# Opening of a trunk layer by feature halves: modulation, weights and the first two projections taken for features 0-511, then for 512-1023

## The reference

```python
sh1, sc1, g1, sh2, sc2, g2 = split(silu(c) @ w_mod + b_mod, 6)     # w_mod: 1024 x 6144, f32
hn   = rms_norm(x, norm1_w) * (1 + sc1) + sh1
proj = hn @ w_in                                                   # w_in: 1024 x 2832, f32
q_a, k_a, v_a, q_m, k_m, v_m, o_m, gates = split(proj, ...)
# attention and a two-direction mLSTM over proj, then @ w_out, x = x + g1 * y
# second norm with sh2, sc2; router over 64 experts (top 8), 192 MB of expert weights, x + g2 * moe
```

## Time and profile before

| what | value |
|---|---|
| median of 3 executions | 644.04 us |
| span of the profiled execution | 642.9 us |
| PE busy | 580.9 us (90% of the span) |
| DVE, ACT, POOL busy | 209.8, 168.1, 33.6 us |
| DMA | 252.55 MB, mean 393 GB/s |
| chain that ended last | PE 63%, DMA 28%, SP's queue 3% |
| mean granted PE clock | 0.975 |

### The profile page before, as it was taken

How to read it: one execution, slowest core, us unless ns; L and a number is a source line. 1 busy time by engine, 2 the same in 40 slices (tenths; PEclk the granted TensorE clock), 3 DMA queues, 4 the chain that set the end, 5 groups by cost and what they waited for, 6 DMA issues and landing times.

```text
span 642.9 us, 11139 instructions
## 1 busy us (share of the span) xinstructions
PE 580.9 (90%) x4568; PEld 405.9 (63%) x4568; DVE 209.8 (33%) x474; ACT 168.1 (26%) x309; POOL 33.6 (5%) x79
## 2 busy tenths in 40 slices
PE   0789999999999999989999999587999999998785
PEld 0478777788867676656675757354567676765352
DVE  0287867787832212011212222020121212121103
ACT  3164726672622121111121212010212121212111
POOL 1240210010100000000000000000000000000002
PEclk9989999999999999999999999788999999999879
DMA  8999599989999899999999999999999999999994
GB/s 334 385 339 392 208 363 383 411 317 396 420 378 374 365 415 411 422 422 420 420 421 422 420 420 421 421 422 421 420 422 421 419 421 421 421 421 420 421 399 168
DMA packets 50662, 252.55 MB, mean 393 GB/s; under 512 B 5912, under 2 KB 11680, under 8 KB 26288
## 3 DMA queue, kind: packets, MB, share of 16 engines
q1 hardware_dynamic: 48240, 246.37, 94.5%
q0 software_dynamic: 1840, 4.21, 2.0%
q10 hardware_dynamic: 528, 1.21, 0.5%
HBM read 250.06 MB, written 1.72 MB: 392 GB/s over the span
## 4 chain that ended last, share of the span: by engine, by line
PE 63%; DMA 28%; SPq 3%; ACT 2%; DVE 2%; issue 1%; POOL 0%; POOLq 0%; DVEq 0%; ACTq 0%
PE bank L1265 22%; PE bank L1341 11%; DMA spare<-in_w_up 7%; PE bank L1236 6%; PE bank L1282 5%; DMA xn<-in_w_up 4%; DMA gb<-in_w_down 4%; DMA ring<-in_w_up 4%; DMA ring<-in_w_in 4%; DMA ring<-in_w_mod 2%; PE bank L834 2%; SPq L617 2%; PE bank L876 2%; PE bank L884 2%; PE bank L880 2%; DMA ccol<-in_c 2%
## 5 line engine op out<-in xcount | busy, mean ns | idle before, releaser
L1265 PE MATMUL bank<-ring,xe 128*64 128x256 f32 (+1 forms) x1680 | 179.4, 398 | 22.9 <-DMA ring<-in_w_up 8.2
L1265 PEld LDWEIGHTS bank<-ring,xe 128*64 128x64 f32 (+1 forms) x1680 | 118.0, 131 | 79.3 <-issue 44.8
L1341 PE MATMUL bank<-ring,actT 128*64 128x512 f32 (+1 forms) x368 | 83.6, 617 | 4.2 <-DVE actT L2313 2.1
L2311 DVE TENSOR_TENSOR act_e<-bank,sil 128x256 f32<-128x256 f32 x26 | 11.0, 424 | 188.2 <-ACT sil L1727 188.2
L2325 DVE SCALAR_TENSOR_TENSOR ylo<-bank,gslot,yhi 128x512 fp32r<-128x512 f32 x50 | 37.5, 750 | 83.6 <-ACT yhi L1740 83.6
L1740 ACT ACTIVATE yhi<-bank,gslot 128x512 fp32r<-128x512 f32 x50 | 34.4, 688 | 116.1 <-PE bank L1341 116.1
L1727 ACT ACTIVATE sil<-bank 128x256 f32<-128x256 f32 x26 | 10.0, 385 | 192.1 <-PE bank L1265 192.1
L1236 PE MATMUL bank<-pone,hhi 128*128 128x256 f32 x200 | 50.0, 288 | 0.0
L1341 PEld LDWEIGHTS bank<-ring,actT 128*64 128x64 f32 (+1 forms) x368 | 24.5, 132 | 39.2 <-issue 38.9
L1236 PE MATMUL bank<-pone,hlo 128*128 128x256 f32 x200 | 48.9, 282 | 0.0
L1722 ACT ACTIVATE xe<-bank 128x512 f32<-128x512 f32 x50 | 29.9, 598 | 48.2 <-PE bank L1236 48.2
(11 more groups left out here) (375 smaller groups left out, 792.0 us busy)
## 6 DMA issues: line engine op xcount, KB each, us to landing
ring<-in_w_gate SPq DMA_DIRECT2D x55, 1024.0 KB, 24.1
ring<-in_w_up SPq DMA_DIRECT2D x50, 1024.0 KB, 25.8
ring<-in_w_down SPq DMA_DIRECT2D x46, 1024.0 KB, 25.8
ring<-in_w_mod SPq DMA_DIRECT2D x12, 2048.0 KB, 13.7
ring<-in_w_in SPq DMA_DIRECT2D x5, 2048.0 KB, 16.1
gb<-in_w_down SPq DMA_DIRECT2D x7, 1024.0 KB, 25.9
gb<-in_w_up SPq DMA_DIRECT2D x5, 1024.0 KB, 21.5
xn<-in_w_gate SPq DMA_DIRECT2D x5, 1024.0 KB, 17.0
```

What stands on the lines that cost most here:

```text
L1265: ins = mm(bank[6][j * w:(j + 1) * w, part * FE:(part + 1) * FE], xe[:, k, slots], weights[:, k, :], start=(k == 0), stop=(k == KD - 1))
L1341: ins = mm(bank[4 + h][j * w:(j + 1) * w, :], actT[:, f, j * w:(j + 1) * w], weights[:, f, 512 * h:512 * h + 512], start=(f == 0), stop=(f ...
```

## The change

The first four ring places now hold: place 0 projection chunk 1, place 1 chunk 0, place 2 shift, place 3 scale. Each is filled and used in two halves of 512 features. A half of shift or scale has all 1024 rows of `w_mod` and 512 of its columns (rows of 2 KB in memory where there were 4 KB). A half of a projection chunk has 512 of its rows. Everything up to the products runs in a loop over f = 0, 1: rows, columns, modulated tokens, upper part and rest of tokens and weights, and four of the eight k-blocks of the products. The products stay open in their PSUM banks from one half to the other. The upper part of chunk 1 and the rest of the tokens move to POOL. ACT makes the tokens of context and the upper part of chunk 0, DVE the latent tokens and the rests. The upper part of chunk 2 is shared between ACT and DVE. POOL's small loads are spread: five of them after the first half, the others after chunk 2 has landed. From load index 6 (chunk 2) on, the order and the places of the loads are as before, and so is PE's order from project(2) on.

Cut to its core:

```diff
@@ loads
-        for what in ("A0", "A1", 1, 0, 2, 3, "g1", 4, "m0", 5, "m1", "g2"):
+        loads = [None] * 6
+        last_use = [None, None, 2, "rH1", "pj1_1", "pj0_1"]
+        proj_chunk = {1: 4, 0: 5}
+        for what in (2, 3, "g1", 4, "m0", 5, "m1", "g2"):
@@ SP
+            load_half_mod(SHIFT, 0, 0, slice(0, KD), chunk_loaded[SHIFT])
+            sp.dma_start(ccol[:, 0, :], t["c_ctx"]...)
+            sp.dma_start(ccol[:, 1, :], t["c"]...)
+            load_scale(0)
+            load_half_chunks(0)
+            sp.wait_ge(chunk_used, 1)
+            load_half_mod(SHIFT, 0, 1, slice(0, KD), chunk_loaded[SHIFT])
+            product(sp, "rH0")
+            load_scale(1)
+            load_half_chunks(1)
+            for i in range(6, N_LOADS):
...
@@ PE
-            transpose_tokens(0)
-            mod_rows("A0")
-            complete("cA0", mod_columns("A0", "cA0"))
-            mod_rows("A1")
-            complete("cA1", mod_columns("A1", "cA1"))
-            transpose_tokens(1)
-            project(1)
-            project(0)
+            shift_rows(0)
+            scale_rows(0, 0)
+            transpose_tokens(0)
+            complete("rH0", scale_rows(0, 1))
+            half_columns(0)
+            project_halves(0)
+            shift_rows(1)
+            transpose_tokens(1)
+            rest_upper_half(0, 0, 1)
+            scale_rows(1, 0)
+            complete("rH1", scale_rows(1, 1))
+            upper_rest_half(0, 0, 0)
+            half_columns(1)
+            upper_rest_half(0, 0, 1)
+            project_halves(1)
+            rest_upper_half(0, 1, 1)
+            for s in range(NST):
+                upper_rest_half(0, 1, s)
             project(2)
+            def half_rows(f, q, blocks):
+                for k in blocks:
+                    for c in range(CT):
+                        ins = mm(ps[r:r + P // CT, P * q:P * q + P], csil[:, k, :], w[:, k, P * c:P * c + P], ...)
+            def project_halves(f):
+                for s in range(NST):
+                    upper_upper_half(1, f, s)
+                for s in range(NST):
+                    upper_rest_half(1, f, s)
+                rest_upper_half(1, f, 0)
+                upper_upper_half(0, f, 0)
+                rest_upper_half(1, f, 1)
+                upper_upper_half(0, f, 1)
+                rest_upper_half(0, f, 0)
@@ ACT
+            for f in range(2):
+                half_rows_out(f)
+                act.wait_ge(ab_ready, f + 1)
+                token_upper(f)
+                token_exact(f)
+                upper_half(f)
@@ DVE
+            V.memset(rows[:, :, :], 0.0)
+            chain(V.memset(gi[:, :, :], 0.0))
+            for f in range(2):
+                half_vectors(f)
+                token_upper(f)
+                rest_half(1, f)
+                token_exact(f)
+                rest_half(0, f)
@@ DVE, after the copy of pj1_0
+            dve.wait_ge(chunk_loaded[proj_chunk[2] % 4], need[proj_chunk[2]])
+            product(dve, "pj1_1")
+            V.tensor_copy(proj_upper(2)[:, 4:8, :], proj_weights(2)[:, 4:8, :]).then_inc(w_upper_part, 1)
@@ POOL
+            first_upper(0)
+            token_rest(0)
             pool.dma_start(bg...)            # and m0, q_norm, k_norm, rope
+            first_upper(1)
+            token_rest(1)
+            pool.wait_ge(chunk_loaded[proj_chunk[2] % 4], need[proj_chunk[2]])
             pool.dma_start(kdup...)          # and caches, biases, router weights, state
```

More of the change, by code:

```diff
@@ L1519, in _ @@
-            act.wait_ge(ab_ready, 1)
-            def token_upper(b):
-                s = b % 2
-                ps = product(act, f"xT{b}")
-                for i in range(4):
-                    k = 4 * (b // 2) + i
-                    ins = A(xhi[:, k, s * P:s * P + P], ps[:, i * P:i * P + P], ACT.Identity,
-                            bias=modc[:, 0, k, s:s + 1], scale=acol[:, k, s:s + 1])
-                ins.then_inc(x_upper[b], 1)
-                act.wait_ge(x_upper[b], 1)
-                act.sem_inc(drained[where[f"xT{b}"]], 1)
@@ L1532, in token_exact @@
-            def token_exact(b):
-                s = b % 2
-                evacuated_once(b)
-                for i in range(4):
-                    k = 4 * (b // 2) + i
-                    ins = A(hT[:, k, s * P:s * P + P], bank[where[f"xT{b}"]][:, i * P:i * P + P], ACT.Identity,
-                            bias=modc[:, 0, k, s:s + 1], scale=acol[:, k, s:s + 1])
-                drain(f"xT{b}", ins)
-            def evacuated_once(b):
-                act.wait_ge(drained[where[f"xT{b}"]], drains[f"xT{b}"] - 1)
@@ L1546, in _, with half_rows_out, upper_half @@
-            token_upper(0)
-            act.wait_ge(chunk_loaded[proj_chunk[1] % 4], need[proj_chunk[1]])
-            A(proj_upper(1)[:, 0:4, :], proj_weights(1)[:, 0:4, :], ACT.Copy).then_inc(w_upper, 1)
-            token_upper(1)
-            for b in (0, 1, 3):
-                token_exact(b)
+            def half_rows_out(f):
+                ps = product(act, f"rH{f}")
+                drain(f"rH{f}", A(rsb[:, f, :], ps[0:MR, 0:2 * P], ACT.Copy))
+            def upper_half(f):
+                half_ready(act, 0, f)
+                k = half_blocks(f)
+                A(proj_upper(0)[:, k, :], proj_weights(0)[:, k, :], ACT.Copy).then_inc(w_upper, 1)
@@ new lines, in token_upper, with token_exact @@
+            def token_upper(f):
+                ps = product(act, f"xT{2 * f}")
+                for i in range(CT):
+                    k = CT * f + i
+                    ins = A(xhi[:, k, 0:P], ps[:, i * P:i * P + P], ACT.Identity,
+                            bias=modc[:, 0, k, 0:1], scale=acol[:, k, 0:1])
+                ins.then_inc(x_upper_act, 1)
+            def token_exact(f):
+                for i in range(CT):
+                    k = CT * f + i
+                    ins = A(hT[:, k, 0:P], bank[where[f"xT{2 * f}"]][:, i * P:i * P + P], ACT.Identity,
+                            bias=modc[:, 0, k, 0:1], scale=acol[:, k, 0:1])
+                ins.then_inc(x_upper_act, 1)
@@ new lines, in token_upper, with token_exact @@
+            def token_upper(f):
+                ps = product(dve, f"xT{2 * f + 1}")
+                for i in range(CT):
+                    k = CT * f + i
+                    ins = V.tensor_scalar(xhi[:, k, P:2 * P], ps[:, i * P:i * P + P],
+                                          acol[:, k, 1:2], modc[:, 0, k, 1:2], ALU.mult, ALU.add)
+                ins.then_inc(x_upper_dve, 1)
+            def token_exact(f):
+                for i in range(CT):
+                    k = CT * f + i
+                    ins = V.tensor_scalar(hT[:, k, P:2 * P], bank[where[f"xT{2 * f + 1}"]][:, i * P:i * P + P],
+                                          acol[:, k, 1:2], modc[:, 0, k, 1:2], ALU.mult, ALU.add)
+                ins.then_inc(x_upper_dve, 1)
```

232 lines of the change are left out of this document (120 added, 112 removed), and 2 rows, old and new, of the table plan.

## The result

The changed kernel takes 646.79 us (median of 20 executions, 645.10 to 648.95); the kernel before, timed beside it, takes 644.61 us (20 executions, 642.82 to 647.50). The ratio is **1.0032**, with a 95% interval of 1.0022 to 1.0043. That is within the 0.5% that the prediction calls "same", but on the slow side: 2.2 us longer where 2.1 us shorter was forecast. The 646.79 us also lie outside the forecast's range of 638.8 to 645.2.

What follows compares the result with a forecast made beforehand. Expert weights on DMA set the later pace, with the opening counted at the scores; 2.6 us from the pause less 0.5 for 2 KB rows gave 642.9 - 2.1 = 640.8 profiled, 641.9 us median, range 638.8 to 645.2.

Steps and rivals of the forecast that it cites:

- What bounds it: Expert weights on DMA set the later pace; the opening's gain counts at the scores, reached last by PE or DMA-ACT-copy.
- PE's path: In the opening, PE about 6 us ahead: loop's last product groups end at 47.3 us, project(2) at 58.5 instead of 64.7.
- the modulation rows: On PE in the opening: 128 matmuls before and after, with 128 columns instead of 256, taken at 45 ns each.
- 2 KB rows: Shift and scale loads: shorter rows cost DMA 0.5 us more for 8.39 MB, bounds 0 and 3.4 us.
- The pause: DMA's first pause, 62 to 68 us at 233 instead of 409 GB/s, goes away: 2.6 us gained.
- 2.6 - 0.5 = 2.1: Pause's gain less the 2 KB rows' price: chunk 4 lands 2.1 us sooner, at 70.6, passing on to the experts.
- and waits 5 us there for ACT: At the scores: PE's own path arrives at 70 us, the scores begin at 75.3; no cost was set for the wait.
- DMA runs dry at chunk 2: Rival: half 0 stays at 1.2 GHz, chunk 2 is asked for at 39.5, DMA loses 6.2 us: 648.1 us; chance 0.11.
- More than the pause: Rival: POOL's reordered small transfers cost DMA less from 26 to 50 us; typically 4 us gained, 640 us; chance 0.22.
- Nothing: Rival: half the cover is missing, or 2 KB rows cost 2 us or more: 643.5 to 645 us; chance 0.12.
- DVE beside POOL: Opening: by a rule, latent rest up to 2.2 us later per half, half 0 1.5 us outside the cover: 643.4 us.
- the cover: Slack hiding new waits in the opening; thinnest 2 us at chunk 2: needed by 33.3 us, PE delivers at 31.2.

Runs made afterwards that it cites:

- e10: The changed kernel unmodified, timed and profiled again: 646.54 us, ratio 1.0025 to the kernel before.
- e9: The changed kernel with 20 identity matmuls filling PE's gap before the scores: 645.31 us, ratio 1.0009 to the kernel before.
- e1: The changed kernel with 26 identity matmuls filling PE's gap before the scores: 645.94 us, ratio 1.0037 to the kernel before.
- e5: The changed kernel with 13 identity matmuls in PE's gap before the scores: 645.52 us, ratio 1.0016 to the kernel before.
- e4: The kernel before with each chunk of shift and scale fetched as two transfers of 512 columns, in 2 KB rows: 647.23 us, ratio 1.0050.
- e12: The kernel before with each chunk of shift and scale fetched as two transfers split over k-blocks, keeping 4 KB rows: 645.43 us, ratio 1.0005.
- e3: The kernel before with ACT rounding five eighths of chunk 4 once more beforehand, which delays the scores: 647.21 us, ratio 1.0053.
- e6: The kernel before with ACT making proj_out(3) and q's copy ahead of the upper part of chunk 4: 645.72 us, ratio 1.0008.
- e8: The kernel before with SP asking for the 1 MB expert tile after chunk 4 instead of before it: 644.45 us, ratio 0.9998.
- e2: The changed kernel with ACT making proj_out(3) and q's copy ahead of the upper part of chunk 4: 641.73 us, ratio 0.9975.
- e7: The changed kernel with SP asking for the 1 MB expert tile after chunk 4 instead of before it: 643.78 us, ratio 0.9981.

## Why the prediction was wrong

**What bounds it: right.** The point to count at was the scores, the two paths to it were PE's and DMA, ACT, copy, and the later one was the second. A shift there does pass to the end, if it is counted behind g1's rows: 1.0 us of the span for each us of the transposes.

**PE's path: right in sign, 6 us forecast, 3.3 us measured.** The first product came at 23.88 (23 forecast), the vectors at 22.2 (21.4). The failed term is the modulation rows. I counted 128 matmuls before and after; the records are 128 before and 256 after, because each instruction takes 128 columns where it took 256, and so there must be twice as many. Groups of 64 took 1.95 us (30 ns each) at full clock, and the first 96 took 4.59 us, so the rows take 9.6 us instead of 5.8. In after's profile chunk 4 was still asked for at 61.24, within the 61.5 that I had set as the limit. In e10, e9, e1 and e5 it was asked for at 61.55, 61.59, 61.99 and 62.35, and landed at 72.1, 72.5, 74.2 and 74.3: the later the ask, the later the landing. Whether the one causes the other isn't shown, so this term may have cost something too.

**2 KB rows: a term that was mis-sized.** I took 0.5 us out of 0 to 3.4, from chunk 4's own 400 against 409 GB/s. e4 measures 2.6 us of the stream with the doubled number of transfers, 1.8 beyond e12, and at the scores 1.6 and 0.7. A transfer alone on an empty queue for two microseconds was a poor guide. In the changed kernel itself the stream is behind by only 0.9 us at 62 us, all of it together. So something gave back what e4 loses beyond that; that POOL's small transfers cost the same wherever they stand is then doubtful, but no run moves them alone.

The Trainium skill's page "DMA: Bandwidth & Descriptors" (Specifications) puts line rate at transfers of 512 B or more. By it 2 KB rows would cost nothing; measured is 384 against 403 GB/s for 2 KB against 4 KB rows at a full DMA share, so here the measurement decides against it.

**The pause: worth less than 2.6 us.** It did vanish. But the stretch of 62 to 64 us that I counted in it was partly the ragged end of the stream, and that end comes back at the end of the longer one: 209 and 12 GB/s before 71.67 in after, 109 and 23 GB/s from 72 to 74 in e5. With chunk 4 queued behind other bytes its landing varies from 71.7 to 74.3 over the profiles of after, e10, e9, e1 and e5, where on an empty queue it landed 7.9 to 8.0 us after its issue in each of before, e3, e4, e6, e8 and e12. Chunk 4 landed 1.1 us sooner in after's profile, not 2.1, and that profile is the best of the five: their mean, 73.0, is no sooner than the 72.74 of before. So the term "2.6 - 0.5 = 2.1" came out between a gain of 1.1 and a loss of 1.6.

**The step that decided: "and waits 5 us there for ACT", priced at nothing.** The idle PE was forecast, in place and releaser; that the clock would drop behind it was not, although showed just that behind 2.45 us of idle time, and I had used it for half 0. The idle time (3.1 to 3.2 us) cost 3.0 us in after's profile, 1.6 in e10's, 1.7 in e3's, and the 1.74 us left in e5's cost 1.6; the profiles of e1, e9, e2 and e7, with the gap filled or at most 1.26 us, paid nothing. Had I priced it by those rows (16 matmuls 3.66 instead of 2.42 us), a loss of 1.2 us or more would have stood against 2.1.

**The rivals.** "DMA runs dry at chunk 2" did not happen: 338 to 388 GB/s in every two microseconds from 26 to 44 us, and the low clock from 26 to 28 us (0.50) was absorbed. "More than the pause" did not either. "Nothing" named the 2 KB rows at 2 us or more, and gave 643.5 to 645; of the three it came nearest. None of them had the clock at the scores.

**DVE beside POOL.** DVE's rest of 2048 columns took 2.93 us beside POOL's token sum, where 2.42 us for 2176 columns gives 2.28, and POOL's sums took 1.27 us each instead of 1.11. The Trainium skill's page "SBUF — State Buffer" (Who interferes with whom) says that a DVE instruction with two SBUF inputs contends with a GpSimd one that reads SBUF, and the trace agrees. It cost DVE 0.65 us a time rather than the 2.2 that I drew from it, since the two overlapped only from 26.96 to 27.74. It lay inside the cover.

**Left open:** how often the clock falls behind a given gap (e5 lost it behind 3.07 us of filling and 1.74 us idle, e7 kept it behind 1.26), why chunk 4 lands at such different times, why profiles of e4, e6 and e8 have a second dip at 170 to 180 us, and how much of after's 2.2 us is rows and how much clock. A kernel with the halves but 4 KB rows was not tried.

## What to carry to other kernels

When an engine is made to arrive earlier at a place where another path decides, ask what its new idle time does: here an early PE lost its clock, and paid more for 3 us of waiting (3.0 and 1.6 us in two profiles) than the change had won at the scores (1.1 and 0.7). Look first whether what it waits for really needs the late transfer; two copies moved ahead on ACT turned 1.0032 into 0.9975. And price a shorter DMA row by a stretch in which the queue is full and such rows are many, not by one transfer on an empty queue.

## What the runs showed of the hardware

- From 4 to 28 us rows of 2 KB moved 384 GB/s where rows of 4 KB in as many transfers moved 403 and in half as many 403 to 406 (before, e3, e6, e8), all at a DMA share of 1.02 to 1.04.
- A PE idle for 3.1 to 3.2 us before the scores was at clock 0.50 within the next microseconds in three profiles of three; the low stretch began at once in after, 1 to 2 us after the scores' start in e10 and e3, and cost 1.6 to 3.0 us.
- Queued behind other bytes, a 2 MB transfer ended at falling rates (209 and 12 GB/s in after, 256 and 92 in e10, 197, 109 and 23 in e5). Against 400 GB/s to the end that is 1.1 to 2.6 us more, by my estimate from these windows, where before's on an empty queue lost 0.8 us so (344 and 41 GB/s).
